# The down product moved behind the turn of the activations in the expert steps of a one-core mixture-of-experts backbone

## The chip, the cores and the metric

The kernel runs on one core of a Trainium2 chip. The metric is the device time of one execution in microseconds (us), as the median of several runs. All data is float32.

## The reference, cut to what matters

Two layers. Each layer has an adaLN modulation, a projection into three groups of heads (a Fourier mixer, differential attention, a gating MLP), an output projection and a layer norm, and after that a grouped top-2 mixture of 16 experts. The change touches the experts alone:

```python
def _moe(h, gates, w1, w3, w2):
    y = jnp.zeros_like(h)
    for e in range(N_EXPERTS):
        a = jax.nn.silu(h @ w1[e]) * (h @ w3[e])
        y = y + gates[..., e:e + 1].astype(h.dtype) * (a @ w2[e])
    return y
```

`h` has 512 rows of 1024 in layer 0 (256 latent and 256 context tokens) and 256 rows in layer 1. `w1[e]` and `w3[e]` are 1024 x 512, `w2[e]` is 512 x 1024, 2 MB each.

## The kernel before, in words

A router picks two experts for each row. The rows are scattered to a table in HBM (`xg_rows`), sorted by expert, in blocks of 32 rows, and an expert takes as many blocks as its rows need (none is left out: an expert has at least one). One block is one **step**. In the trace there are 41 steps in layer 0 and 25 in layer 1. At the end of a layer the results are gathered from a second table (`y_rows`), weighed and added.

The engines are programmed apart and joined by semaphores, all with the number of the step. For step s they do:

- TensorE (PE) `turn_rows` (L1791): four transposes that turn the block of the step after, s + 1, so that its columns lie on the partitions. `up` (L1802): 32 matmuls of 32 rows with w1 and w3, four side by side in column tiles of 32 (`tile_position`), each in two float32 passes, so 64 MATMUL records. `turn_act` (L1809): two full transposes of the result, so that the halves that w1 and w3 gave lie beside each other. `down` (L1817): 16 matmuls with w2, also in column tiles of 32, 32 records.
- VectorE (DVE) `copy_up` (L1366) takes `up`'s result out of PSUM, `rows_out` (L1369) the turned rows of s + 1, `copy_out` (L1376, in `last_out`) the down product of step s - 1, and `product` (L1373) multiplies the two halves of step s. They stand in this order. In layer 0 the first three steps have `beside(n)` behind them, the residual of the attention block on whole tiles (L1101, L1103).
- ScalarE (ACT) stages rows for the step after next (L772) and takes the silu of step s, `gate` (L946).
- GpSimd (POOL) loads the rows of a block (L697) and stores the results (L701).
- SyncE (SP) loads the weights into a ring of three experts: w1 and w3 of expert e once `up_done` says that expert e - 3 is through its up products, w2 once `down_done` says the same of its down products (`follow`, L588).

TensorE's order is written out in `rest` and `expert`: `up` of step s, then `rest`: `turn_rows` of s + 1, `down` of s - 1, `turn_act` of s, then `up` of s + 1. `rest` is unrolled at each place in which it is called. Between `turn_act` and the next `up` stand only instructions of PE's sequencer: a nest of `Fori` and `If` (L1848 to L1857), since the number of steps of an expert is known only at run time, and for the first step of the next expert the waits of `first_up` (L1827, L1828). `turn_act` waits for `copy_up` of its own step (`up_copied`). `down` waits for w2, for `product` of step s - 1 and for the copy of the down product before it.

Of the kernel before, what the change touches and what calls it, by code (L numbers as in the profile page):

```python
# [275 lines left out]
def backbone(nc, x, c, ctx, c_ctx, w_ada, b_ada, w_in, w_fourier, diff_lambda, diff_subln, sgu_ln_g, sgu_ln_b,  # L276
# [8 lines left out]
    with es:  # L285
# [144 lines left out]
        up_copied = per_layer("up_copied")  # L430
# [25 lines left out]
        def wait_apart(eng, semaphore, value):  # L456

            eng.wait_ge(semaphore, value)
            eng.sem_inc(passed, 1)
# [42 lines left out]
        def expert_full(p, n):  # L502
            return w_full[3 * p + n] if p < 2 else lent_full[n]

        def expert_fills(L, p, n, round_):

            base = RING_BASE[L][3 * p + n] if p < 2 else ROUNDS * L
            if L + 1 == DEPTH and (p, n) == (0, 0):
                base -= 1
            return round_ * 16 + 16 * (base + 1)  # L510
# [937 lines left out]
        def _(pe):  # L1448
# [82 lines left out]
            for L in range(DEPTH):  # L1531
# [256 lines left out]
                def turn_rows():  # L1788
                    turned = XG.rearrange("s (d k) -> s k d", k=4)
                    for k in range(4):  # L1790
                        mm = pe.transpose(ROWS_PS[:, 2 * ROWS * k:2 * ROWS * k + 2 * ROWS], turned[:, k, :],  # L1791
                                          IDENT[0:2 * ROWS, 0:2 * ROWS])
                    mm.then_inc(rows_turned[L], 1)
# [12 lines left out]
                def turn_act():  # L1806
                    turned = EXU.rearrange("s (f k) -> s k f", k=2)
                    for k in range(2):
                        mm = pe.transpose(TURN_PS[:, P * k:P * k + P], turned[:, k, :], IDENT)  # L1809
                    mm.then_inc(act_turned[L], 1)  # L1810

                def down(p):
                    for k in range(FE // P):
                        rows = ATX[:, k % 2, ROWS * (k // 2):ROWS * (k // 2) + ROWS]
                        for q in range(4):
                            o = ROWS * q
                            mm = pe.matmul(DOWN_PS[o:o + ROWS, 0:256], rows,  # L1817
                                           moe_down(p)[:, k, 256 * q:256 * q + 256],
                                           start=(k == 0), stop=(k == FE // P - 1), tile_position=(0, o))
                    mm.then_inc(down_done[L], 1)  # L1820
# [10 lines left out]
                def rest(p, step, p_down, round_):  # L1831

                    wait_apart(pe, rows_staged[L], step + 2)
                    turn_rows()
                    if p_down is not None:
                        pe.wait_ge(expert_full(p_down, 2), expert_fills(L, p_down, 2, round_))
                        pe.wait_ge(product_ready[L], step)
                        pe.wait_ge(out_copied[L], step)
                        down(p_down)
                    pe.wait_ge(up_copied[L], step + 1)  # L1840
                    turn_act()

                def expert(e, p, step, before, own, after, more=None):

                    fixed = isinstance(e, int)
                    following = steps_before(pe, L, e + 1)
                    rest(p, step, None if fixed else (p - 1) % 3, before)
                    with pe.If(following > step + 1):  # L1848
                        with pe.Fori(0, 3) as a:
                            square = a * a  # L1850
                            with pe.If(following > square + (step + 1)):
                                with pe.Fori(0, (square - a if T > 2 else 0) + 1) as b:
                                    begin = square + b * 5 + 1
                                    with pe.If(following > begin + step):
                                        with pe.Fori(0, a * 2 + 1) as c_:
                                            j = begin + c_
                                            with pe.If(following > j + step):  # L1857
                                                pe.wait_ge(xgt_ready[L], step + j + 1)
                                                up(p, fixed and L + 1 == DEPTH)
                                                rest(p, step + j, p, own)  # L1860
                                            with pe.Else():
                                                pe.nop()
                                    with pe.Else():
                                        pe.nop()
                            with pe.Else():
                                pe.nop()
                        pe.nop()
# [52 lines left out]
```

## Time and profile before

| | |
|---|---|
| median of 3 runs | 1198.59 us (1198.38 to 1199.21) |
| the profiled execution's own time | 1196.56 us |
| its span, first to last instruction | 1194.9 us |
| mean granted TensorE clock | 0.924 |
| PE busy (matmul) | 987.1 us, 83% of the span |
| PE weight loads (PEld), beside it | 557.9 us, 47% |
| DVE, ACT, POOL busy | 27%, 19%, 22% |
| experts of layer 0, first `up` to last `down` | 356.2 to 676.1 us |
| experts of layer 1 | 918.4 to 1158.2 us |

PE counts as busy from the start of a matmul to its modelled end. The weight loads of a matmul run beside the matmuls in front. Instructions of a sequencer (branches, register arithmetic, waits) do not count as busy; in the profile they are marked with a q (PEldq), and time in which an engine waited for nothing that the profile shows is called issue. The granted clock is 1.00 at 2.4 GHz and 0.5 at 1.2 GHz.

### The profile page before, as it was taken

What the parts mean: (1) busy time and instruction counts of PE and PEld (TensorE: products, weight loads), DVE (VectorE), ACT (ScalarE), POOL (GpSimd) and SP (SyncE); (2) the same over time, 40 slices, a digit from 0 to 9 for tenths busy, and PEclk for the clock granted to TensorE, in tenths of its full rate; (3) what the DMA queues carried; (4) which work ended last, traced back from release to release, by engine and by line L of the source; (5) the groups of instructions that cost most, each with busy time, mean ns of one, the idle gap of its engine ahead of it and who ended that gap; (6) DMA issues with size and microseconds to landing.
All of it is one profiled execution on the core that took longest, in us unless ns stands there. A gap on an engine that the chain in (4) does not pass through costs nothing.

```text
span 1194.9 us, 23782 instructions
## 1 busy us (share of the span) xinstructions
PE 987.1 (83%) x9029; PEld 557.9 (47%) x9030; DVE 326.3 (27%) x766; ACT 225.7 (19%) x556; POOL 258.1 (22%) x483
## 2 busy tenths in 40 slices
PE   3999999999999989988985549998988768756870
PEld 1444555564565545555542324645546445424440
DVE  1003032733335212222220166014333312111215
ACT  0311011760231111111110123103512001000100
POOL 0200000010025433343431330000102223311441
PEclk9899999999989999999997869999997889977995
DMA  9995474572354894679999948537574999999952
GB/s 337 360 403 232 140 283 152 201 286 102 141 201 135 283 348 146 244 292 400 390 389 409 390 167 294 179 133 280 232 298 163 392 394 399 392 405 408 396 194 106
DMA packets 89125, 331.42 MB, mean 277 GB/s; under 512 B 10796, under 2 KB 13052, under 8 KB 64500
## 3 DMA queue, kind: packets, MB, share of 16 engines
q1 hardware_dynamic: 66516, 282.13, 61.7%
q0 software_dynamic: 21088, 47.48, 11.3%
q10 hardware_dynamic: 1472, 1.12, 0.3%
q8 instruction: 34, 0.56, 0.2%
q14 instruction: 15, 0.12, 0.0%
HBM read 303.18 MB, written 27.53 MB: 277 GB/s over the span
## 4 chain that ended last, share of the span: by engine, by line
PE 71%; DMA 14%; issue 7%; DVE 4%; ACT 1%; SPq 1%; POOL 1%; POOLq 0%; DVEq 0%; ACTq 0%
PE PS L1802 18%; PE PS L1562 16%; DMA W<-in_moe_w 11%; PE PS L1817 8%; PE PS L1724 7%; PE PS L1495 3%; PE PS L1791 3%; PE PS L1528 3%; PE PS L1578 3%; PE PS L1809 2%; DMA W<-in_w_ada 2%; PE PS L1674 2%; PE PS L1771 1%; PE PS L1686 1%; PE PS L1735 1%
## 5 line engine op out<-in xcount | busy, mean ns | idle before, releaser
L1802 PE MATMUL PS<-W,EX 128*32 128x256 f32 x2912 | 182.5, 403 | 59.4 <-DMA W<-in_moe_w 32.2
L1562 PE MATMUL PS<-W,XT 128*128 128x512 f32 (+1 forms) x480 | 188.8, 553 | 2.4 <-ACT XT L797 2.4
L1802 PEld LDWEIGHTS PS<-W,EX 128*32 128x32 f32 x2912 | 97.1, 116 | 127.9 <-issue 77.4
L1562 PEld LDWEIGHTS PS<-W,XT 128*128 128x128 f32 x480 | 91.1, 191 | 95.3 <-issue 92.9
L670 POOL TENSOR_TENSOR RSTD<-VAR,HALF 128x1 f32<-128x1 f32 (+1 forms) x24 | 16.3, 683 | 454.6 <-DVE VAR L1076 454.6
L772 ACT ACTIVATE AT<-EX 64x512 f32<-64x512 f32 x64 | 40.4, 631 | 387.0 <-PE PS L1791 365.4
L1366 DVE COPY EX<-PS 128x256 f32<-128x256 f32 x66 | 28.0, 424 | 302.2 <-PE PS L1802 302.2
L1802 PE MATMUL PS<-RAB,EX 128*32 128x256 f32 x640 | 82.3, 414 | 32.8 <-DMA XT<-in_moe_w 19.3
L701 POOL DMA_DIRECT2D y_rows<-AT x136 | 67.4, 497 | 165.0 <-DVE AT L1376 155.3
L701 POOL DMA_DIRECT2D y_rows<-EX x128 | 63.5, 496 | 144.1 <-DVE EX L1376 131.0
L1817 PE MATMUL PS<-W,AT 128*32 128x256 f32 x1472 | 89.3, 382 | 1.5 <-DVE AT L1373 1.5
L1724 PE MATMUL PS<-W,XT 128*128 128x512 f32 x192 | 83.2, 593 | 0.0
L1802 PE MATMUL PS<-XT,EX 128*32 128x256 f32 x640 | 81.7, 414 | 0.0
L697 POOL DMA_DIRECT2D EX<-xg_rows x136 | 67.8, 500 | 54.9 <-issue 36.6
L797 ACT ACTIVATE XT<-PS,MB,MA 128x128 f32<-128x128 f32 x112 | 40.6, 470 | 132.1 <-PE PS L1528 132.1
L1802 PEld LDWEIGHTS PS<-RAB,EX 128*32 128x32 f32 x640 | 39.8, 119 | 54.7 <-issue 35.0
L1817 PEld LDWEIGHTS PS<-W,AT 128*32 128x32 f32 x1472 | 43.9, 109 | 28.1 <-issue 1.8
L1724 PEld LDWEIGHTS PS<-W,XT 128*128 128x128 f32 x192 | 36.2, 190 | 44.0 <-issue 44.0
L1791 PEld LDWEIGHTS PS<-C,AT 64*128 64x128 f32 x272 | 37.6, 209 | 36.8 <-issue 36.8
L1791 PE MATMUL PS<-C,AT 64*128 64x64 f32 x272 | 46.7, 292 | 7.6 <-issue 7.5
L1528 PE MATMUL PS<-C,X 128*128 128x128 f32 x112 | 16.9, 300 | 32.3 <-DVE X L1095 32.3
L1802 PEld LDWEIGHTS PS<-XT,EX 128*32 128x32 f32 x640 | 38.4, 119 | 7.9 <-issue 5.1
(206 smaller groups left out, 1057.0 us busy)
## 6 DMA issues: line engine op xcount, KB each, us to landing
W<-in_moe_w SPq DMA_DIRECT2D x65, 2048.0 KB, 19.6
W<-in_w_ada SPq DMA_DIRECT2D x24, 2048.0 KB, 12.3
RAB<-in_moe_w SPq DMA_DIRECT2D x10, 2048.0 KB, 18.9
XT<-in_moe_w SPq DMA_DIRECT2D x10, 2048.0 KB
H<-in_moe_w SPq DMA_DIRECT2D x10, 2048.0 KB, 19.7
W<-in_w_in SPq DMA_DIRECT2D x7, 2048.0 KB, 21.0
EX<-xg_rows POOLq DMA_DIRECT2D x136, 64.0 KB, 5.7
W<-in_w_out SPq DMA_DIRECT2D x4, 2048.0 KB, 20.0
```

The costliest lines, as they stand in the source:

```text
L697: pool.dma_start(XRAW[b][ROWS * q:ROWS * q + ROWS, :], part_of_rows(xg_rows, n, slice(512 * q, 512 * q + 512))) .then_inc(rows_in[b][L], 16)
L701: pool.dma_start(part_of_rows(y_rows, n, slice(256 * q, 256 * q + 256)), YO[b][ROWS * q:ROWS * q + ROWS, :]) .then_inc(y_written[b][L], 16)
L772: nc.scalar.activation(dst, src, ACT.Copy).then_inc(done, 1)
L797: ins = nc.scalar.activation(XT[:, n, P * t:P * t + P], ps[:, P * k:P * k + P], ACT.Identity, bias=MB[:, kind, n, t // 2:t // 2 + 1], scal ...
L1495: pe.matmul(ps[32 * n:32 * n + 32, :], CT[:, k, :], w[n][:, k, :], start=(k == 0), stop=False, tile_position=(0, 32 * n))
L1528: mm = pe.transpose(ps[:, P * n:P * n + P], piece, IDENT)
L1562: mm = pe.matmul(ps[:, 0:cw], XT[:, k, P * t:P * t + P], w[:, k, :], start=(k == 0), stop=(k == KD - 1))
L1578: mm = pe.matmul(ps, XT[:, k, P * t:P * t + P], w[:, k, :], start=(k == 0), stop=(k == KD - 1))
L1724: mm = pe.matmul(ps, XT[:, k, P * t:P * t + P], w[:, k, :], start=(k == 0), stop=(k == KD - 1))
L1791: mm = pe.transpose(ROWS_PS[:, 2 * ROWS * k:2 * ROWS * k + 2 * ROWS], turned[:, k, :], IDENT[0:2 * ROWS, 0:2 * ROWS])
L1802: mm = pe.matmul(UP_PS[o:o + ROWS, 0:256], rows, w[:, 256 * a:256 * a + 256], start=(k == 0), stop=(k == KD - 1), tile_position=(0, o))
L1817: mm = pe.matmul(DOWN_PS[o:o + ROWS, 0:256], rows, moe_down(p)[:, k, 256 * q:256 * q + 256], start=(k == 0), stop=(k == FE // P - 1), tile ...
```

## The change

In `rest` the wait for `up_copied` and `turn_act` go ahead of the waits of `down` and `down` itself. Nothing else differs.

```diff
                     wait_apart(pe, rows_staged[L], step + 2)
                     turn_rows()
+                    pe.wait_ge(up_copied[L], step + 1)
+                    turn_act()
                     if p_down is not None:
                         pe.wait_ge(expert_full(p_down, 2), expert_fills(L, p_down, 2, round_))
                         pe.wait_ge(product_ready[L], step)
                         pe.wait_ge(out_copied[L], step)
                         down(p_down)
-                    pe.wait_ge(up_copied[L], step + 1)
-                    turn_act()
```

The order on TensorE at the end of the first step of an expert (layer 0; a MATMUL row with a wait shows the semaphores it waits for, `- ` is before and `+ ` the change):

```order
 L1791 MATMUL PS<-C,AT 128x64 x3
-L1836 ISA
+L1835 REGISTER_ALU
+L1809 MATMUL PS<-C,EX 128x128 [waits up_copied0]
+L1809 MATMUL PS<-C,EX 128x128
+L1838 ISA
 L1817 MATMUL PS<-W,AT 32x256 [waits out_copied0,product_ready0,w_full2]
 L1817 MATMUL PS<-W,AT 32x256 x15
-L1840 REGISTER_ALU
-L1809 MATMUL PS<-C,EX 128x128 [waits up_copied0]
-L1809 MATMUL PS<-C,EX 128x128
 L1848 COMPARE_AND_BRANCH
```

The two transposes with their wait went from behind the 16 down matmuls to the place ahead of them; the branch of L1848 now follows the down matmuls.

The order on TensorE at the end of a further step of the same expert, inside the loops, up to where the branches lead on:

```order
 L1791 MATMUL PS<-C,AT 128x64 x3
+L1809 MATMUL PS<-C,EX 128x128 [waits up_copied0]
+L1809 MATMUL PS<-C,EX 128x128
 L1817 MATMUL PS<-W,AT 32x256 [waits out_copied0,product_ready0,w_full2]
 L1817 MATMUL PS<-W,AT 32x256 x15
-L1809 MATMUL PS<-C,EX 128x128 [waits up_copied0]
-L1809 MATMUL PS<-C,EX 128x128
 L1857 UNCONDITIONAL_BRANCH
```

The same move; what stands next to the branches is again `down` in place of `turn_act`. The order on DVE, ACT, POOL and SP is as before.

## Rows read from the trace of the kernel before

**Rows 1.** The page, part 4: shares of the chain that ended last

```profile
PE 71%; DMA 14%; issue 7%; DVE 4%; ACT 1%; SPq 1%; POOL 1%; POOLq 0%; DVEq 0%; ACTq 0%
```

**Rows 2.** Windows: stretch, length, busy PE, PEld, DVE, ACT, POOL, clock, DMA share, GB/s

```profile
532.00:666.00 134.00, 105.54 (x1572) 60.37 (x1568) 25.06 (x64) 14.53 (x32) 45.41 (x92) 0.94 1.01 393
931.00:1093.00 162.00, 113.60 (x1532) 66.05 (x1532) 28.86 (x66) 13.78 (x31) 48.69 (x98) 0.86 1.02 398
```

**Rows 3.** The chain in order of time, layer 0: start us, us, what

```profile
409.40 0.62 PE PS L1791 x4
410.02 1.86 PE PS L1817 x32
411.88 0.44 PE PS L1809 x2
412.32 3.59 PE PS L1802 x64
...
418.83 1.46 issue
```

**Rows 4.** PE's waits and its L1809 in 387 to 532.1, 649.7 to 675 and 1093 to 1158 us

```profile
PE PS L1802 <- issue: 10.1, 10, 2.3
...
L1809 PE MATMUL PS<-C,EX x40: 283/334/386, 390.3 to 527.3; 128*128 128x128 f32 x40
...
PE PS L1802 <- issue: 1.5, 1, 1.5
...
PE PS L1802 <- issue: 5.8, 4, 2.2
...
L1809 PE MATMUL PS<-C,EX x16: 283/334/386, 1102.1 to 1155.1; 128*128 128x128 f32 x16
```

**Rows 5.** Timeline of layer 0's first step, without down: start us, us, engine, line, operation

```profile
360.57 0.69 PE L1791 MATMUL PS<-C,AT 64*128 64x64 f32 x4
360.72 0.42 DVE L1366 COPY EX<-PS 128x256 f32<-128x256 f32 x1 [6.63 <-PE PS L1802]
361.20 0.51 PE L1809 MATMUL PS<-C,EX 128*128 128x128 f32 x2
```

**Rows 6.** PE's sequencer, L1848 in 361.19 to 361.21 us, L1857 in 367.90 to 367.91 us

```profile
L1848 PEldq COMPARE_BRANCH  x1: 89/89/89, 361.2 to 361.2; - x1
...
L1857 PEldq COMPARE_BRANCH  x1: 193/193/193, 367.9 to 367.9; - x1
```

**Rows 7.** L1857's first branch (410.43 to 410.44 us); L1817's weight loads, 409.94 to 410.43 us

```profile
L1857 PEldq COMPARE_BRANCH  x1: 174/174/174, 410.4 to 410.4; - x1
...
L1817 PEld LDWEIGHTS PS<-W,AT x16: 106/110/110, 409.9 to 410.4; 128*32 128x32 f32 x16
```

**Rows 8.** Timeline, DVE, PE and its weight loads beside the residuals of layer 0, 366 to 384.3 us

```profile
367.44 0.42 DVE L1366 COPY EX<-PS 128x256 f32<-128x256 f32 x1
...
368.58 0.32 PEld L1809 LDWEIGHTS PS<-C,EX 128*128 128x128 f32 x2 [0.41 <-issue]
...
376.88 0.42 DVE L1376 COPY EX<-PS 128x256 f32<-128x256 f32 x1 [1.47 <-PE PS L1817]
377.60 0.29 DVE L1373 TENSOR_TENSOR AT<-PS,EX 128x128 f32<-128x128 f32 x1 [0.29 <-ACT EX L946]
...
382.60 0.42 DVE L1366 COPY EX<-PS 128x256 f32<-128x256 f32 x1
...
384.21 0.42 PE L1802 MATMUL PS<-W,EX 128*32 128x256 f32 x4 [0.44 <-issue]
```

**Rows 9.** Timeline at the end of layer 1's experts

```profile
1155.20 0.42 DVE L1376 COPY EX<-PS 128x256 f32<-128x256 f32 x1 [1.61 <-PE PS L1817]
...
1156.41 2.27 POOL L701 DMA_DIRECT2D y_rows<-EX  x4 [3.58 <-DVE EX L1376]
```

**Rows 10.** Timeline of PE: two up products of layer 0 behind gaps of 2.3 us

```profile
443.17 5.35 PE L1802 MATMUL PS<-W,EX 128*32 128x256 f32 x64 [2.30 <-issue]
...
537.24 3.66 PE L1802 MATMUL PS<-W,EX 128*32 128x256 f32 x64 [2.25 <-issue]
```

## The prediction, made before the changed kernel had run

> **What bounds the kernel now.** I read the shares of the chain first: 71% of it is PE and 14% DMA [rows 1], so what the change does to TensorE's own order reaches the end unless a transfer stands between. The windows say where that is so [rows 2]: the DMA engines are busy without a break (a share over 1.00) from 532 to 666 us in layer 0 and from 931 to 1093 us in layer 1. There the weights stream, up products wait for landings, and a TensorE step that is a little longer or shorter costs nothing. PE itself bounds three stretches: layer 0 up to 532 us (where the end of an up product starts the stream, so all delay up to there is passed on whole), the last two turns of layer 0, from 649.7 us on, behind the last landing that PE waits for there, and layer 1 from 1093 us.
>
> Then one step in the chain [rows 3]: `turn_rows` 0.62, `down` 1.86, `turn_act` 0.44, `up` 3.59, with either nothing or an idle gap before `up` ("issue", 1.46 us at 418.83). I call a turn without a gap A and one with a gap B. PE's waits count them [rows 4]: 10 gaps in the 20 turns of 387 to 532 us (40 transposes, two a step), so 10 A and 10 B; behind 649.7 us one A and one B; and from 1093 us 4 gaps in 8 steps, one of which is the last, so 3 A and 4 B. In all 14 A and 15 B.
>
> **Part 1: the new wait.** `turn_act` now comes right behind `turn_rows`, when DVE has hardly taken `up`'s result. The first step of each layer has no down product and shows this order already [rows 5]: the copy starts 0.15 us behind `turn_rows` and takes 0.42, and `turn_act` starts 0.63 us behind `turn_rows`, where a down product starts 0.62 behind. The wait costs 0.01 us a step: its cover is `turn_rows`. With the cover gone it would cost what DVE is late, which happens in part 4.
>
> **Part 2: the A turns.** An up product of 64 passes takes 3.59 us, a down product of 32 takes 1.86 [rows 3]. The 32 passes more cost 3.59 - 1.86 = 1.73 us, so a group of four costs 0.22, and 1.86 - 1.73 = 0.13 us is lost once in each of the two, where the column tiles of 32 give way to a full transpose. Before, both `up` and `down` end that way. After, `down` is followed by `up`, in the same tiles, and one of the two losses goes. A turn is 0.62 + 1.86 + 0.44 = 2.92 us before and 0.63 + 0.44 + 1.73 = 2.80 after: 0.12 to 0.13 us less. 14 x -0.13 = **-1.8 us**.
>
> The Trainium skill (TensorEngine Tiling, Key Properties) says that changing the tiling mode, not just the tile, drains TensorE. By that rule one of the step's drains goes, as the sum has it; the trace agrees that there is a loss and puts it at 0.13 us.
>
> **Part 3: the B turns.** What ends a gap is PE's sequencer: the branches of the loop nest and the waits of `first_up` have to be through before the next `up` can be handed over. So it matters when the sequencer gets to the first branch. Two rows say what holds it. It stands still at a wait: in the first step its branch comes at 361.2, the very time at which `turn_act` is released, and in the next step at 367.9 [rows 6], just behind the end of a late copy at 367.44 + 0.42 = 367.86 [rows 8], though the transposes themselves ran only at 368.58 [rows 8]. And it runs ahead of the array by a limited amount: the first branch at 410.43 comes when 16 of the 32 weight loads of `down` have started, 0.49 us behind its first [rows 7]. Left in the queue are then 8 down matmuls (two passes each) and 2 transposes, ten in all. After the change ten in the queue are ten down matmuls, so the branch comes when 6 of 16 are off, three groups of four passes, 0.49 - 0.22 = 0.27 us behind `down`'s start. From `turn_rows` that is 0.63 + 0.44 + 0.27 = 1.34 us, against 0.62 + 0.49 = 1.11 before. The branches take as long as ever, so each B turn is 0.23 us longer. In the A turns, where they were hidden, I assume that they stay so; one that does not is longer by up to 0.23 us in place of 0.13 shorter. 15 x 0.23 = **+3.4 us**. Bounds: 0, if the queue is no limit; and 0.45 (+6.7 us), if it counts passes and not matmuls (16 + 2 = 18 passes left, so the branch comes one group later). I take 0.23, since it is what the queue holds in instructions, and a pass is no instruction in the order of the program.
>
> **Part 4: the late copies of layer 0.** `beside` puts residuals on DVE in front of the copy. In step 1 the copy ends at 367.86 [rows 8]. Before, `down` ran meanwhile, and only the sequencer was held. After, `turn_act` waits for it, `down` starts 0.44 later, the branch 0.27 behind that: +0.71 us. In step 3 two residuals stand ahead. `copy_out` of step 1 now starts 0.45 us later, so it ends at 377.75 for 377.30, and the product that came at 377.60 (waiting for ACT) comes at 377.82: residuals and copy are 0.22 later. From the copy's end (382.60 + 0.42 + 0.05 = 383.07) to the next up at 384.21 it was 1.14 us; now 0.44 + 1.73 = 2.17 stand there, the array's own work. +0.22 + 2.17 - 1.14 = +1.25. Together **+2.0 us**. Layer 1 has its residuals ahead of a stretch that waits for weights: nothing.
>
> **Part 5: the end of a layer.** The last `copy_out` but one starts POOL's row of stores (copy at 1155.20, stores from 1156.41 [rows 9]), and the stores, not the last down product, lead on to the gather. That `down` now starts 0.44 + 0.01 later behind `turn_rows`: 2 x 0.45 = **+0.9 us**. The very last `down` waits for a product that stands behind this copy_out on DVE and comes some 0.3 us later, hidden behind POOL's 2.27 us of stores.
>
> **What is moved past what.** No DMA issue moves in its queue. SP waits for `down_done`, 0.45 us later at each step; its load of w2 joins a stream that never runs dry from 532 us on, and ahead of that w2 is long there before its use. ACT's staging waits for `turn_rows`, which is where it was. `gate` and `product` have the whole next `up` of 3.59 us to hide in. All at nothing.
>
> **Sum.** -1.8 + 3.4 + 2.0 + 0.9 = +4.5 us: 1196.56 becomes 1201.1 for the profiled execution. The median of the runs is 2.03 us above that execution, 1198.59, so the forecast is **1203.1 us**, 0.4% slower. Some 0.2% (2.4 us) is what a measurement here can tell from no change. With the bounds of part 3 the forecast's own range is 1199.7 to 1206.4.
>
> **Rivals.**
>
> *The queue is no limit.* The sequencer would hand over all of `turn_act` and `down` at once when the copy is done, and the B turns would cost nothing: -1.8 + 1.25 + 0.9 = +0.4 us (in step 1 the 0.71 goes too), 1199.0 us, no change. For it: nothing shows the queue's end directly. Against: the branch at 410.43 came 0.49 us behind `down`'s start with nothing to wait for. The Trainium skill (TensorE: Matmul & The Clock Gate, Architectural detail) gives TensorE's queue a depth of 64; by that figure `down` would fit in whole and this rival would be the result, but the row speaks for some ten matmuls with their loads. Chance 0.14.
>
> *Faster: the tiling change costs more than the 0.13 us, and the gap hangs on the array.* The weight loader stands idle 0.41 us at the tiling change [rows 8], which is the other reading of the price. If all of it were won, and if the branches began only when the array is through with what is handed over, so that the gap moves along unchanged, all 29 turns would win: 29 x -0.41 = -11.9, with +1.25 + 0.9 that is -9.7 us, 1188.9 us. It decides from 0.16 us a turn on (29 x 0.16 = 4.6, less the 2.15 of parts 4 and 5, makes the 2.4 us that can be told). Against it: passes would have to come out 0.3 us shorter than their own spacing, and the branch of 410.43 was well ahead of the array. Chance 0.08.
>
> *More stretches at the low clock.* Behind the gap of 2.30 us that ends at 443.17 the up product took 5.35 us, at 1.2 GHz for most of it; behind one of 2.25 us at 537.24 it took 3.66, at 2.4 GHz throughout [rows 10]. After the change PE's idle gap in a B turn is 0.23 + 0.13 = 0.36 us longer, and step 1 has 1.2 us of idle and a long gap in a row. Each stretch more costs 5.35 - 3.66 = 1.7 us; two of them give 1206.5 us. One that goes, since the gap falls elsewhere, gives 1.7 back: it is no case of its own, but part of the range. Chance 0.18.
>
> **How the numbers follow.** Forecast 0.60, rivals 0.14, 0.08 and 0.18. The forecast falls within 0.2% only if its B turns cost next to nothing or a low-clock stretch goes: 0.03 of it. Slower by over 0.2%: 0.57 + 0.18, with some of the first rival's chance 0.77; within 0.2% 0.15; faster 0.08. The range, 1198.8 to 1207.6 us, holds the first rival, the forecast with its bounds and two to three low-clock stretches, and leaves out the faster case.
>
> **What would show it.** In the profile after: `turn_act` 0.63 us behind `turn_rows` in nearly every step; `up` 1.73 behind `down` in half of the turns; a step without a gap 0.13 us shorter than the 6.51 of before; gaps between the end of `down` and `up` some 0.36 us longer than those between `turn_act` and `up`; the branches' first 0.27 us behind `down`'s start; `turn_act` in step 1 and 3 of layer 0 released by DVE, 1.2 and about 2 us late; the landing-bound up products of 634 and 649 us later by the 3 us or so that layer 0 has lost by 532; layer 1 unshifted against its own start until 1093. I am wrong if the B gaps stay as long as they were, if A turns are shorter by 0.3 us or more, or if the streams of weights show holes that they did not have.

## The result, and the profile after

The changed kernel takes 1211.67 us (median; 1209.58 to 1213.09) against 1198.88 for the kernel before: a ratio of 1.0113, 95% interval 1.0089 to 1.0137, or 13.5 us more. It is slower, as forecast, but by three times the +4.5 us of the sum, and outside the range. The profiled execution took 1209.58 us (span 1207.9, granted clock 0.920) against 1196.56 (1194.9, 0.924), so the two traces are 13.0 us apart and can be compared place by place.

The page after, shares of the chain; it answers to [rows 1] and tells only that PE has a point less, and idle "issue" time and DVE a point more each:

```profile
PE 70%; DMA 14%; issue 8%; DVE 5%; ACT 1%; SPq 1%; POOL 1%; POOLq 0%; DVEq 0%; ACTq 0%
```

So I laid the starts of the up products of both traces beside each other, each counted from its own layer 0's first up product (356.17 us before, 354.83 after, ahead of anything that the change touches), and read where the distance grows:

| place (time before, us) | distance so far | grown here | what lies there |
|---|---|---|---|
| 391.30 | +4.21 | +4.21 | opening of layer 0: two late copies, a gap turn, a stretch at the low clock |
| 537.24 | +7.81 | +3.60 | 10 turns with a gap, 10 without |
| 666.82, last up of layer 0 | +10.64 | +2.83 | two slow up products, stream of weights |
| 918.43, first up of layer 1 | +10.89 | +0.25 | |
| 1093.47 | +11.31 | +0.42 | stream of layer 1 |
| 1148.85, last up | +13.97 | +2.66 | four gap turns, one slow up product |
| end of the span | +14.35 | +0.38 | last stores, gather |

The last distance is the 13.0 us of the spans and the 1.35 us by which the first up product came earlier.

**A turn.** The chain of the changed kernel in layer 0 (start us, us, what), which answers to [rows 3]:

```profile
412.69 0.62 PE PS L1791 x4
413.31 0.43 PE PS L1809 x2
413.75 1.86 PE PS L1817 x32
415.61 3.45 PE PS L1802 x64
419.06 0.62 PE PS L1791 x4
419.68 0.43 PE PS L1809 x2
420.12 1.86 PE PS L1817 x32
421.98 1.93 issue
```

`turn_act` starts 0.62 behind `turn_rows`, as forecast, and a turn with a gap takes 0.62 + 0.43 + 1.86 + 1.93 = 4.84 us to the next up product, where [rows 3] had 0.62 + 1.86 + 0.44 + 1.46 = 4.38. That is +0.46 a gap turn and not +0.23. Across the ten gap turns up to 537 us the starts move apart by 0.40 to 0.47 each, 4.32 in all. The waits of PE in the same stretch (393 to 538.3 us), for [rows 4]:

```profile
PE PS L1802 <- issue: 14.5, 10, 2.7
```

Still ten gaps, 4.4 us more in sum. In layer 1 from 1106 us on it is `7.5, 4` for the `5.8, 4` of [rows 4], 0.43 each.

**The sequencer.** Its first branch behind `turn_rows` of 404.79 us, and the weight loads of `down` that have started by then, for [rows 7]:

```profile
L1857 PEldq COMPARE_BRANCH  x1: 179/179/179, 406.3 to 406.3; - x1
...
L1817 PEld LDWEIGHTS PS<-W,AT x15: 106/109/110, 405.8 to 406.2; 128*32 128x32 f32 x15
```

A pass is a weight load with its matmul. 15 of the 32 passes are off and 17 are left, 0.48 us behind `down`'s start. Before it was 16 left and the 2 transposes behind them: 18. Over all steps with a down product the count is 17 in 56 of 64 turns after (16 in the others) and 18 in 61 of 64 before. That fits a limit in passes; in matmuls of the program the same counts are ten before and eight or nine after.

**The opening of layer 0.** Timeline, PE (start us, us, engine, line, operation, and in brackets the idle time before), and a window of it (columns as in [rows 2]); they answer to [rows 8]:

```profile
366.56 0.50 PE L1809 MATMUL PS<-C,EX 128*128 128x128 f32 x2 [1.13 <-DVE EX L1366]
...
367.00 1.93 PE L1817 MATMUL PS<-W,AT 128*32 128x256 f32 x32
...
382.79 0.51 PE L1809 MATMUL PS<-C,EX 128*128 128x128 f32 x2 [1.79 <-DVE EX L1366]
383.23 2.94 PE L1817 MATMUL PS<-W,AT 128*32 128x256 f32 x32
```

```profile
384.00:387.40 3.40, 3.40 (x40) 1.75 (x36) 0.62 (x2) 0.00 (x0) 0.25 (x1) 0.50 0.00 0
```

Both late copies now hold the array, as forecast. What was not in the sum: right behind the 1.79 us of idle the granted clock falls to 0.50 (1.2 GHz) for 3.4 us, and `down` takes 2.94 where the row of step 1, at 367.00, has 1.93.

**543 us.** The up product that answers to [rows 10]'s second row, and a later one; then SP's queue around the first of them, after and then before:

```profile
543.70 5.35 PE L1802 MATMUL PS<-W,EX 128*32 128x256 f32 x64 [2.68 <-issue]
...
560.43 5.35 PE L1802 MATMUL PS<-W,EX 128*32 128x256 f32 x64 [1.98 <-issue]
```

```profile
538.33 0.37 SPq L545 DMA_DIRECT2D RAB<-in_moe_w  x1
...
552.03 0.37 SPq L545 DMA_DIRECT2D H<-in_moe_w  x1
```

```profile
532.30 0.37 SPq L545 DMA_DIRECT2D RAB<-in_moe_w  x1
...
543.44 0.37 SPq L545 DMA_DIRECT2D H<-in_moe_w  x1
```

Behind a gap of 2.68 us the first ran at 1.2 GHz for most of its time, where behind 2.25 it had run at 2.4. The second did so behind 1.98 us. The load of w2 waits for the `down` behind it, so it goes out 13.70 us behind the load of w1 instead of 11.14, and the DMA engines run out of work just then:

```profile
551.50:553.50 2.00, 2.00 (x44) 1.06 (x36) 0.62 (x2) 0.00 (x0) 0.05 (x1) 1.00 0.55 119
```

The share of 0.55 stands in a stream that, by my forecast, never ran dry. At the end of layer 1 the timeline shows what the prediction had in part 5. First the `turn_rows` of before, 2.76 us ahead of the copy in [rows 9], then the changed kernel, where it is 3.19:

```profile
1152.44 0.69 PE L1791 MATMUL PS<-C,AT 64*128 64x64 f32 x4
```

```profile
1165.07 0.69 PE L1791 MATMUL PS<-C,AT 64*128 64x64 f32 x4
...
1168.26 0.42 DVE L1376 COPY EX<-PS 128x256 f32<-128x256 f32 x1 [2.05 <-PE PS L1817]
```

### The profile page after: what moved, and what is told of

Its sections match the earlier page's. It is cut to its first block, busy times and chain, and to the rows that moved or that the text cites. A ratio compares the mean times of both kernels' runs of the same rounds, so it can differ in the third digit from the quotient of the medians.

```text
span 1207.9 us, 23782 instructions
## 1 busy us (share of the span) xinstructions
PE 988.7 (82%) x9029; PEld 563.8 (47%) x9030; DVE 320.3 (27%) x766; ACT 218.6 (18%) x556; POOL 257.2 (21%) x483
## 4 chain that ended last, share of the span: by engine, by line
PE 70%; DMA 14%; issue 8%; DVE 5%; ACT 1%; SPq 1%; POOL 1%; POOLq 0%; DVEq 0%; ACTq 0%
PE PS L1802 17%; PE PS L1562 16%; DMA W<-in_moe_w 11%; PE PS L1817 8%; PE PS L1724 7%; PE PS L1495 3%; PE PS L1791 3%; PE PS L1528 3%; PE PS L1578 3%; PE PS L1809 2%; DMA W<-in_w_ada 2%; PE PS L1674 2%; PE PS L1686 1%; PE PS L1771 1%; PE PS L1735 1%
## 5 line engine op out<-in xcount | busy, mean ns | idle before, releaser
L1817 PE MATMUL PS<-W,AT 128*32 128x256 f32 x1472 | 90.1, 385 | 1.9 <-DVE AT L1373 1.9
L1817 PEld LDWEIGHTS PS<-W,AT 128*32 128x32 f32 x1472 | 44.2, 110 | 31.5 <-issue 3.4
```

What stands on the lines that cost most here:

```text
L1817: mm = pe.matmul(DOWN_PS[o:o + ROWS, 0:256], rows, moe_down(p)[:, k, 256 * q:256 * q + 256], start=(k == 0), stop=(k == FE // P - 1), tile ...
```

## The experiments

My theory after the result: the loss sits in the turns with a gap, since the sequencer reaches its branches later, and in the opening; the turns without a gap pay nothing. The rival: every step pays about the same, whatever ends it (an effect of the array, or of DVE's and ACT's later starts). All gap turns stand behind the second or a later up product of an expert, so the two can be parted by where the new order is applied.

### e1 and e2: the new order behind an expert's first up product only, or behind its others only

```diff
-    def rest(p, step, p_down, round_):
+    def rest(p, step, p_down, round_, inner, fixed):
+        act_first = not inner      # e1; in e2: act_first = inner
         wait_apart(pe, rows_staged[L], step + 2)
         turn_rows()
+        if act_first:
+            pe.wait_ge(up_copied[L], step + 1)
+            turn_act()
...
-        pe.wait_ge(up_copied[L], step + 1)
-        turn_act()
+        if not act_first:
+            pe.wait_ge(up_copied[L], step + 1)
+            turn_act()
```

> The new order only behind the first up product of an expert, the old one behind its further steps. Theory 1 (the branches start later behind the down product, and only turns whose branches are not hidden pay): every turn with a gap comes behind a further step, so nothing is paid but the later stores at the end of the two layers, 0.9 us: +1 us against before, 0 to +2.5. Theory 2 (each step pays alike, for the wait and for the later down_done): 31 of 64 turns, +6 us.

> The new order only behind the further steps of an expert, the old one behind the first. Theory 1: all the gaps (some 14 x 0.43 = 6 us) and the late copies of expert 0 in layer 0 (3 us) are still paid, the ends of the layers are not: +8 to +11 us. Theory 2: 33 of 64 turns, +6.5 us.

Measured: e1 1.0016 (1.0002 to 1.003), +1.9 us; e2 1.0106 (1.0084 to 1.0129), +12.7 us. Together 14.6, the change's 13.5 within the intervals. The rival, with the loss in equal halves, falls. In e1's trace the distance to the kernel before stays within 0.24 us up to 618 us; at the end it is 3.9, of which 1.6 come with an up product at the low clock at 1134.36, behind a gap of 2.25 us. In the chain of e1 both orders stand one behind the other, first the old one with its gap, then the new one, without:

```profile
414.34 0.62 PE PS L1791 x4
414.96 1.86 PE PS L1817 x32
416.82 0.44 PE PS L1809 x2
417.26 1.48 issue
...
422.40 0.62 PE PS L1791 x4
423.02 0.44 PE PS L1809 x2
423.45 1.86 PE PS L1817 x32
```

e2 shows the gap of the change, on the inner step alone:

```profile
424.48 0.62 PE PS L1791 x4
425.10 0.43 PE PS L1809 x2
425.54 1.86 PE PS L1817 x32
427.40 1.91 issue
```

e2 came out over its +8 to +11, and its trace shows no such excess: of the 12.7 us between the two spans 4.1 lie ahead of the first up product of layer 0 (360.27 us for 356.17), where the two kernels are the same, and the other 8.7 behind it. Its distance is 4.09 us at 391.30 and 7.98 at 537.24, so the opening, which has a stretch at the low clock here too, and the gap turns have their full price, as in the changed kernel (4.21 and 7.81). But the up product of 543 us (549.32 in this trace) ran at 2.4 GHz here, behind a gap of 2.74, and the stream of weights lost nothing: at 634.63, where an up product waits for a landing, the distance is 7.21, less than at 537.24. The changed kernel, with the slow up product, has 9.08 there, more than its 7.81.

### e3: the old order in expert 0 only

```diff
+        act_first = not fixed      # fixed: expert 0 (steps 0 to 4 in layer 0)
```

> The new order everywhere but in expert 0, which keeps the old one. Theory 1 with the late copies as a cost of their own: 3 to 4 us less than the change in full, +9 us against before. If the late copies are nothing apart from the gaps (theory 2, 5 of 64 turns spared): +12 us.

Measured: 1.0063 (1.0042 to 1.0084), +7.5 us, 6.0 less than the change; the expectation had some 1.5 us more left. The distance is 0.05 at 391.30 for the change's 4.21, and grows to 2.44 by 537.24 and 3.47 at 634.63. So the opening costs 4 us at its place. The whole time differs by about 6, three times what part 4 gave it; but in e3's trace the up product of 443 us, slow in the kernel before and in the changed one, ran at 2.4 GHz, and that is 1.7 us of the difference.

### e5: the old order, with the sequencer held up and nothing else

```diff
                     pe.wait_ge(up_copied[L], step + 1)
                     turn_act()
+                    if inner:
+                        for _ in range(4):
+                            wait_apart(pe, rows_staged[L], 1)
```

> The order of the kernel before, with four waits that are always satisfied (about 0.1 us each on TensorE's sequencer) between turn_act and the branches, behind the further steps of an expert. No data wait, no down product and no store moves. Theory 1 (branches that start some 0.4 us later are what the gaps pay): 14 x 0.4 = +6 us, with the holes in the weight stream and low clock that follow up to +9; the gaps in the trace longer by 0.4. Theory 2 (the loss comes from what the other engines deliver): 0 to +1.

Measured: 1.0155 (1.0135 to 1.0174), +18.5 us, far over +6 to +9. The chain, at the same place:

```profile
420.52 0.62 PE PS L1791 x4
421.14 1.86 PE PS L1817 x32
423.01 0.44 PE PS L1809 x2
423.44 2.12 issue
425.56 5.35 PE PS L1802 x64
```

The order on the array is the old one to the hundredth, and the gap is 2.12 for 1.46 all the same. So a later sequencer is enough to lengthen a gap turn by just as much as it is late. The four waits (each long satisfied, and each with an increment of a counter in the same instruction) took 0.61 to 0.65 us together, not the 0.4 I had taken; 14 turns of 0.65 make 9.1 us, and the turns without a gap stay within 0.02. The other 9 come in single turns, most with an up product at the low clock: the one behind this gap took 5.35 us, and its turn moved the distance by 1.69 us instead of nothing; up to the products of 377, 451, 543, 588 and 604 us (times of before) single turns do the like, by 1.2 to 2.9 us, and the granted clock over the span is 0.911 for 0.924. I did not separate the clock from the holes in the stream. That the loss outgrows the delay is what the changed kernel shows too.

### e6: `turn_act` between the two halves of `down`

```diff
-                        down(p_down)
+                        down(p_down, range(0, 2))
                     pe.wait_ge(up_copied[L], step + 1)
                     turn_act()
+                    if p_down is not None:
+                        down(p_down, range(2, 4))
```

> turn_act between the two halves of down. Theory 1 with a queue of some 17 passes: the first branch can come only when the first half is off, from turn_rows on 0.62 + 0.99 + 0.1 = 1.7 us against 1.11 before and 1.53 after, so the gap turns are 0.6 us longer than before, more than in the change itself (0.43), though turn_act stands half way: +9 to +14 us. If the place of turn_act is what costs: half of the change, +6 to +7 us.

Measured: 1.027 (1.0248 to 1.0292), +32.3 us: two to three times the expected. The chain at that place:

```profile
421.89 0.62 PE PS L1791 x4
422.51 1.00 PE PS L1817 x16
423.51 0.43 PE PS L1809 x2
423.94 1.00 PE PS L1817 x16
424.95 2.32 issue
```

The halves take 2.00 for 1.86 in one piece, a change of tiling more at 0.14 us. That is the 0.13 of part 2, seen from the other side. The gap turn is 5.37 us, 1.0 over the old 4.38. Its first branch comes just as the second half starts, with 12 of its passes left and not 17. I expected 0.6 from a limit of 18; why it waits for longer here I can't say. The steps without a gap are split too: each has the second 0.14 against it, and those behind an expert's first up product lose 0.5.

### e4 and e10: `down` first, then `turn_rows` and `turn_act`

If the limit is what is left behind the last wait, the opposite move should gain: with `down` in front, only six passes stand behind it, and the branch comes while `down` still runs. e10 is the same kernel as e4 in a second series, and the trace read here is its own.

```diff
                 def rest(p, step, p_down, round_):
-                    wait_apart(pe, rows_staged[L], step + 2)
-                    turn_rows()
                     if p_down is not None:
...
                         down(p_down)
+                    wait_apart(pe, rows_staged[L], step + 2)
+                    turn_rows()
                     pe.wait_ge(up_copied[L], step + 1)
```

> A third order: down, turn_rows, turn_act, so that 11 passes of down and the six transposes stand in the queue when the branches start. Theory 1: the first branch comes some 0.2 us earlier behind up than in the kernel before, the gaps are 0.2 us shorter (15 of them, -3 us), up follows down's tiling without a change (-0.13), turns without a gap wait 0.15 us for rows_out (+2), the layers end 0.6 us earlier each (-1.2): -2 us against before, -4 to +1. Theory 2 (waits and down_done): down_done comes earlier and up_copied is never waited for, so -1 to -2 us from the ends alone, the gaps as they were.

> The kernel of e4 once more, for an undisturbed profile. Theory 1: the first branch behind an up product comes 0.49 us earlier than in the kernel before (18 passes queued: 12 of down and the 6 transposes), gap turns 0.45 us shorter, turns without a gap within 0.05 us; about -3 us against before, -5 to -1. Theory 2: gaps as before.

Measured: 0.9976 (0.9962 to 0.999), -2.9 us, and in the second series 0.9969 (0.9955 to 0.9982), -3.7 us. Faster than the kernel before, as expected. e10's chain:

```profile
413.58 1.73 PE PS L1817 x32
415.31 0.64 PE PS L1791 x4
415.94 0.02 issue
415.96 0.44 DVE EX L1369
416.40 1.13 issue
```

`down` takes 1.73, as it follows `up` in the same tiles. The branches end 1.73 + 0.64 + 0.02 + 0.44 + 1.13 = 3.96 us behind the end of `up`, where it was 4.38: -0.42, and -0.42 to -0.48 across the gap turns (e4's expectation had 0.2). The first branch comes 0.49 us earlier from the up product's last load, with 12 passes of `down`, 4 and 2 transposes left: 18 again. Seven of the ten turns without a gap up to 537 us are within 0.02 us of the old ones, although `down` is 0.13 shorter, since DVE's copy (L1369), which was hidden behind `down`, now stands on the path.

### e7, e8, e9: the residuals of layer 0 off the opening

In `beside` the residuals stood ahead of the copies of steps 1 and 3; here they come behind DVE's loop over the steps. e7 does it to the changed kernel, e8 to e4's, e9 to the kernel before.

```diff
-                    beside(n)
+                    if n == 0:
+                        beside(n)
...
                     step(0)
+                for n in range(3):
+                    residuals(n)
```

(with `load_ln(L, 1)` behind the issues of the first gathers, since it waits for them)

> The changed kernel with the residuals of the attention block behind the expert loop on VectorE, instead of behind its first three steps; the load of the next norm's vectors goes behind the gathers' issue. If the late copies of steps 1 and 3 cost what e3 says (5 us with the low clock behind them): 5 us less than the change, +8 us against before; turn_act in steps 1 and 3 starts 0.62 us behind turn_rows. If it was the order of expert 0 for another reason: no gain.

> down, turn_rows, turn_act, and the residuals behind the loop. The order alone gave -3 us; the late copies held the sequencer in the kernel before too, by 0.8 us in step 1 and 1.9 in step 3: -5 to -6 us against before. If the late copies cost nothing where turn_act stands last: -3 us.

> The order of the kernel before with the residuals behind the expert loop. The late copies hold TensorE's sequencer in steps 1 and 3 of layer 0 there too: -2 to -3 us against before. With that, e8's -7.4 us would be the order's -3 us, the residual's -2 to -3, and 1 to 2 us that only both give. If late copies cost nothing where turn_act stands last: 0, and e8 is the order alone in another spread of runs.

Measured: e7 1.0053 (1.0032 to 1.0073), +6.3 us, 7 us less than the change; e8 0.9938 (0.9916 to 0.9959), -7.4 us; e9 1.0004 (0.9992 to 1.0016), no change. In e7's timeline the wait of step 1 is gone:

```profile
364.41 0.69 PE L1799 MATMUL PS<-C,AT 64*128 64x64 f32 x4
...
365.09 0.50 PE L1817 MATMUL PS<-C,EX 128*128 128x128 f32 x2
```

0.68 us behind `turn_rows`, and the distance at 391.30 is -0.39 where the change had +4.21. With e3 that makes two independent removals of the opening's loss: 4.2 and 4.6 us at its place, 6.0 and 7.2 in the medians. Here too the up product of 443 us ran at 2.4 GHz, 1.7 us that are not the opening's.

e9 missed its -2 to -3. In its trace the opening gains 1.1 us, which is nearly all that was there to gain: in the kernel before step 3 kept the array idle for 0.44 us only ([rows 8], at 384.21). Its up product of 543 us runs at 1.2 GHz, in the old order and behind a gap of 2.27 (+1.7 us), and 4.3 us are lost between the last up product of layer 0 and the first of layer 1. The residuals stand there now, but in e7 too, which loses only 0.3 there; 1.7 of the 4.3 is the last up product at 1.2 GHz. That execution took 1203.50 us, 6.5 above the kernel's median, so the two losses are in part its own and don't explain the median. The gain of e8 over e4's order (3.7 to 4.5 us) is not e9's: why the residuals' place is worth something in that order and nothing in the old one stays open. The two traces show where: e8 is 1.5 us ahead of e10 at 391.30, and 1.6 more at 451, where the up product of 443 us ran at 2.4 GHz and e10's at 1.2. **e8 beats both kernels**: 1188.83 us against 1196.28 for the kernel before in the same series.

## Why the prediction was right or wrong

**Part 1, the new wait: right.** 0.62 us behind `turn_rows` in nearly every step, covered by it.

**Part 2, the turns without a gap: right in price, half in count.** Of the ten up to 537 us five came 0.11 to 0.14 us shorter. The other five, those behind an expert's first up product, changed by -0.06 to +0.02: there the branches came out from under the array, as the text allowed for single turns and then did not sum. -0.7 us instead of -1.3 in this stretch. The second rival, 0.3 us or more a turn, fell with it.

**Part 3, the gap turns: the mis-sized term.** "Ten in the queue are ten down matmuls" was wrong. The counts of 18 before, 17 after and 18 in e10 fit passes (in matmuls of the program they are ten, eight or nine, and twelve), so the bound of 0.45 that I had worked out and put aside was the value: measured 0.43 in the median. 15 turns of it are 6.5 us, not 3.4. I had chosen by what a matmul is in the program, though the row showed passes. e1, e2, e5 and e10 show the mechanism from four sides: nothing without a gap, all of it with one, the same from waits alone, and the opposite sign when the branch comes earlier. Counted from the last weight load of the up product, the first branch comes at 1.63 us before, and 0.49 earlier in e10, 0.43 later in the change, 0.61 in e5 and 0.97 in e6; the gap turns are 0.47 shorter and 0.43, 0.65 and 1.00 longer (medians of the ten up to 537 us). That the branch's time sets the gap is shown. That a limit in passes sets the branch's time is what fits three orders; e6's 12 does not fit it and stays open. The Trainium skill (TensorE: Matmul & The Clock Gate, Architectural detail) gives the queue a depth of 64; by that figure nearly all of `down` would have been taken in at once, and no turn here shows it. First rival: fallen.

**Part 4, the late copies: right in place, nearly in size, but not alone.** Step 1 cost +1.02 for the 0.71; 0.21 of the difference is part 3's term again (the branch 0.48 behind `down`'s start, not 0.27). Step 3 cost +2.16, of which some 1.0 is `down` at half the clock, so 1.2 for the 1.25. What I left out is the turn behind it, which has a gap too (0.45), and the low clock: 3.40 us at half speed are 1.7 us. 4.2 us at the place in all.

**Part 5, the ends of the layers: half.** 0.43 for 0.45 at the end of layer 1, and the span grows by 0.38 there. At the end of layer 0 nothing like it can be told: from its last up product to layer 1's first the distance grows by 0.25 in all.

**"A stream that never runs dry": wrong.** It did in 551.5 to 553.5 us. The load of w2 was 2.56 us later behind that of w1: the gap turn 0.45, `down` in it 0.45 later, and the slow up product 1.7. The last up product of layer 0 that waits for a landing, at 649.67, has slipped by 2.4 us against 537.24. In the seven other traces of the experiments in which the product of 543 us was slow (e3, e5 to e10) this slip is 0.7 to 4.7 us; in e1 and e2, where it was not, 0.3. The slow up product is not the new order's own doing alone, since e9 had it.

**The clock, third rival: it came on top of the forecast and not in its place.** Four stretches that the kernel before did not have at these places: at 384 (1.7 us), 543.7 (1.7), 561.5 (1.1) and 1145.2 (behind a gap of 2.60 us; 1.6, of which 0.5 comes back in the product of 1093 us, slow in both kernels but for less of its time in the changed one). I had priced a stretch rightly and made of it a case of 0.18. [rows 10] (2.30 fell, 2.25 did not) looks like an edge that longer gaps would cross, but the length of the gap alone does not decide. Three rows, from the changed kernel, e2 and e10:

```profile
1027.34 3.66 PE L1802 MATMUL PS<-W,EX 128*32 128x256 f32 x64 [2.65 <-issue]
```

```profile
549.32 3.66 PE L1802 MATMUL PS<-W,EX 128*32 128x256 f32 x64 [2.74 <-issue]
```

```profile
530.98 5.35 PE L1802 MATMUL PS<-W,EX 128*32 128x256 f32 x64 [1.91 <-issue]
```

The stretch of the opening is the change's own by more than one trace: the two kernels whose array waits for both late copies (the change and e2) have it, and the kernel before, e1, e3, e7 and e9 do not. The products of 543 and 1144 us (the 26th and the 64th) were slow in eight of the eleven traces each, in e9's old order too (gaps of 2.27 and 2.20 us). How much of those stretches is the change's and how much the single execution's is not shown.

The sum by what was measured, in the two traces: gap turns 6.9 (16 of 0.43), turns without one -1.0, late copies 2.2, clock where PE bounds 2.8 (1.7 in the opening, 1.1 net in layer 1), ends 0.4, stream of layer 0 2.4, between the layers and in layer 1's stream 0.7: 14.4 for 14.35 us. The forecast of 4.5 missed 3.5 us in the gap turns, 3.0 in the streams and what lies between them, and 2.8 in the clock, the last two put at nothing. The slow up product of 543 us is at most 1.7 of the stream's 2.4, and the parts of the stream were not tested one by one.

## What to carry to other kernels

Where a nest of branches stands behind TensorE work and shows as "issue" ahead of the next product, count what is handed over behind the last wait: the branches began when 17 or 18 passes were left (12 in e6), so here the long product belonged in front of the waits and the short transposes behind them (e4 and e10: -2.9 and -3.7 us, where the change made it +13.5). And when a change lengthens many gaps of some 2 us, behind which the granted clock falls in some places and not in others, a low-clock stretch or two and what waits for them belong into the sum with their chance, not among the rivals.

## What the runs showed of the hardware that I had not expected

- TensorE's sequencer ran some 17 to 18 float32 passes (load and matmul) ahead of the weight loader in the kernel before, the changed one and e10; in e6, with transposes inside the run of passes, it was 12 in every turn.
- Four satisfied semaphore waits in a row on TensorE's sequencer, each with an increment, took 0.61 to 0.65 us, about 0.16 each (e5).
- Each run of float32 passes in column tiles that gives way to transposes costs 0.13 to 0.14 us more than one that goes on in the same tiles: one such end less in the change and in e10, one more in e6.
- The gap's length did not tell whether the granted clock fell to 0.50 behind it, for about 3.4 us and 1.6 to 1.7 us of time each. In the eleven traces, from the sixth up product of layer 0 on, it was low for over 2 us of the up product behind 1 of 153 gaps of 0.5 to 1.75 us, behind 29 of 85 of 1.75 to 2.25, and behind 29 of 40 longer ones up to 3.2; 2.76 us left it at 1.0 in e3 and e7. In the opening it fell behind 1.79 us, in the change and in e2, with another idle stretch of 1.13 two steps earlier in the changed kernel.
